# A streaming encoder layer on one NeuronCore: where the conv rows of odd tiles are put in the opening stage, and how x transposed is stored

## What is computed

```
h = rmsnorm(x);  z = h @ w_in            # q, k, v, forget logits, GLU input, memory queries, 3 gates
A = forgetting attention (8 heads x 64)  @ w_fox_o
B = swish(layernorm(causal depthwise conv, width 31, of the GLU)) @ w_conv_o
C = cross attention into 256 memory tokens (4 heads x 128) @ w_mem_o
merged = gate0 * A + gate1 * B + gate2 * C     # gates = sigmoid(h @ w_in[:, C_G:]), 3 x 1024 columns
x = x + merged @ w_out
x = x + PEER(rmsnorm(x))    # 8 heads, top 16 of 128 x 128 experts; rows u[idx], v[idx] of 1024 floats
```

## Time and profile before

| | us |
|---|---|
| device time, median of 3 runs | 4222.19 (4215.44 to 4236.77) |
| device time of the profiled execution | 4211.38 |
| its span, first to last instruction | 4209.6 |
| TensorE busy | 3368.6 (80%) |
| VectorE busy | 2713.5 (64%) |
| GpSimd busy | 2386.7 (57%) |
| ScalarE busy | 1073.8 (26%) |
| data moved | 1321 MB, 314 GB/s on average |

### The profile page before, as it was taken

One profiled execution on the slowest core, in us unless ns is written; L12 is line 12 of the kernel. 1 busy time (PEld: TensorE's weight loads), 2 busy tenths in 40 slices (PEclk: granted clock), 3 DMA queues, 4 the chain that ended last, 5 costly groups with the idle time before them and its releaser, 6 DMA issues.

```text
span 4209.6 us, 34861 instructions
## 1 busy us (share of the span) xinstructions
PE 3368.6 (80%) x9706; PEld 1700.1 (40%) x9706; DVE 2713.5 (64%) x6240; ACT 1073.8 (26%) x2515; POOL 2386.7 (57%) x2341
## 2 busy tenths in 40 slices
PE   8898799897898687777768777776877777687787
PEld 7786454543443343333323333333333333233332
DVE  4599561676776566666666666666666666666674
ACT  5222672223421122112121222212222221222221
POOL 5230340354554366666666666666666666667665
PEclk9999899998999798988989899998988999998998
DMA  6334636798899699999999999999999999999998
GB/s 214 84 90 116 181 109 217 271 315 289 285 343 316 242 363 367 372 360 359 372 362 367 369 367 370 363 372 373 364 368 369 369 366 373 363 378 362 367 362 308
DMA packets 462958, 1321.27 MB, mean 314 GB/s; under 512 B 67802, under 2 KB 134518, under 8 KB 462767
## 3 DMA queue, kind: packets, MB, share of 16 engines
q0 software_dynamic: 313344, 1140.99, 72.1%
q1 hardware_dynamic: 148058, 173.45, 13.1%
q10 hardware_dynamic: 1365, 4.60, 0.3%
HBM read 1275.31 MB, written 43.55 MB: 313 GB/s over the span
## 4 chain that ended last, share of the span: by engine, by line
POOL 22%; PE 13%; issue 12%; DMA 8%; another core or an unknown queue 7%; DVE 5%; ACT 1%; DVEq 0%; POOLq 0%; ACTq 0%
POOL late_u_rows L2129 11%; POOL late_v_rows L2137 11%; PE late_sums_ps L2250 10%; DMA late_u_rows<-in_peer_u,late_expert_idx 4%; DMA late_v_rows<-in_peer_v,late_expert_idx 3%; DVE late_u_rows L2483 2%; PE late_q_ps L2172 1%; PE late_h_T_ps L2154 1%; ACT late_diag L2298 0%; ACT L2287 0%; PE late_h_T_ps L2161 0%; PE late_scores_ps L2188 0%; DVE late_one_hot L2416 0%; DVE late_x L2492 0%
## 5 line engine op out<-in xcount | busy, mean ns | idle before, releaser
L2250 PE MATMUL late_sums_ps<-late_v_rows,late_diag 128*128 128x512 f32 (+1 forms) x3392 | 1742.2, 652 | 487.2 <-DMA late_v_rows<-in_peer_v,late_expert_idx 264.2
L2483 DVE CUSTOM_DVE_ANT_0 late_u_rows<-late_u_rows,late_rows_ps 128x1024 f32<-128x1024 f32 x960 | 1167.3, 1216 | 701.5 <-DMA late_u_rows<-in_peer_u,late_expert_idx 595.9
L2250 PEld LDWEIGHTS late_sums_ps<-late_v_rows,late_diag 128*128 128x128 f32 (+1 forms) x3392 | 655.5, 204 | 1450.8 <-issue 1366.4
L2137 POOL DMA_INDIRECT late_v_rows<-in_peer_v,late_expert_idx x896 | 863.3, 963 | 570.3 <-issue 254.3
L2129 POOL DMA_INDIRECT late_u_rows<-in_peer_u,late_expert_idx x896 | 882.0, 984 | 320.4 <-issue 258.2
L2298 ACT ACTIVATE late_diag<-identity,late_weights 128x128 f32<-128x128 f32 x784 | 271.0, 390 | 798.3 <-DMA open_gain<-in_norm_w 373.5
L1593 POOL DMA_INDIRECT open_u_rows<-in_peer_u,late_expert_idx x128 | 158.4, 1237 | 349.7 <-DVE late_dots L1954 229.2
L2304 ACT ACTIVATE late_gelu<-late_dots 128x4 f32<-128x4 f32 x240 | 48.9, 204 | 971.1 <-issue 577.7
L1968 DVE SCALAR_TENSOR_TENSOR late_x<-open_v_rows,late_weights,late_x 128x1024 f32<-128x1024 f32 x128 | 164.4, 1284 | 115.8 <-issue 94.7
L1128 POOL TENSOR_SCALAR attn_probs<-attn_probs,attn_row_scale 128x256 f32<-128x256 f32 (+2 forms) x68 | 93.2, 1377 | 197.5 <-DVE attn_row_scale L1239 197.4
L481 POOL TENSOR_TENSOR front_w_lower<-front_w_raw,front_w_upper 128x512 fp32r<-128x512 f32 x62 | 95.1, 1553 | 193.2 <-ACT front_w_upper L685 192.0
(11 more groups left out here) (376 smaller groups left out, 4380.3 us busy)
## 6 DMA issues: line engine op xcount, KB each, us to landing
open_weight_columns<-in_w_in SPq DMA_DIRECT2D x96, 256.0 KB
late_u_rows<-in_peer_u,late_expert_idx POOLq DMA_INDIRECT x896
late_v_rows<-in_peer_v,late_expert_idx POOLq DMA_INDIRECT x896
front_w_raw<-in_w_in SPq DMA_DIRECT2D x48, 256.0 KB, 5.6
scr_m<-open_gated SPq DMA_DIRECT2D x42, 256.0 KB
open_weight_columns<-in_peer_w_q SPq DMA_DIRECT2D x32, 256.0 KB
w_mem_o<-scr_m SPq DMA_DIRECT2D x14, 512.0 KB
late_h<-scr_xT SPq DMA_DIRECT2D x12, 512.0 KB
```

Source lines behind the costliest of these rows:

```text
L2137: pool.indirect_dma_start(v[m % V_RING][:], None, io["peer_v"][0], bass.IndirectOffsetOnAxis(ap=rows_of(m), axis=0)).then_inc(s_v[m % V_RI ...
L2250: ins = pe.matmul(acc[0:rows, h, :], diag[k % DIAGS][:, 0:rows], v[n % V_RING][:, h * BANK:(h + 1) * BANK], start=(at == 0), stop=(n == ti ...
L2483: dve.tensor_tensor_reduce(u[n % U_RING][:], u[n % U_RING][:], h2_rows, 1.0, 0.0, ALU.mult, ALU.add, dots[:, n % COLS:n % COLS + 1]).then_ ...
```

## The change

Three edits. The DRAM scratch of x transposed gets a leading tile axis, `(NT + 1, P, KC, P)`, so that a tile of 128 tokens is one run of 1024 floats (4096 bytes) per partition, in the stores of the front and in the loads of the opening (25 loads; for the sample tile, of 64 rows, runs stay 64 floats). The conv rows of odd units go to tile 0's columns of `foxT`. And `load_conv(9)` is issued in SyncE's turn u = 2, after a wait for the routing of head 2, instead of in turn u = 7; the loads of units 10 to 15 stay where they were.

```diff
 def store_whole(xi):
-    sp.dma_start(scr["xT"][:, :, xi * P:xi * P + n], whole[xi % X_RING][:, :, 0:n])
+    sp.dma_start(scr["xT"][xi, :, :, 0:n], whole[xi % X_RING][:, :, 0:n])
...
-conv_rows = [L.memT[:, :, 0:P], w_mem[:, 2, 0:BANK].rearrange("p (j t) -> p j t", j=CT)]
+conv_rows = [L.memT[:, :, 0:P], L.foxT[:, :, 0:P]]
...
 def load_xT(u):
-    sp.dma_start(x_T[u % 2][:, :, 0:rows], scr["xT"][:, :, t * P:t * P + rows])
+    sp.dma_start(x_T[u % 2][:, :, 0:rows], scr["xT"][t, :, :, 0:rows])
...
-sp.dma_start(O.mT[:], scr["xT"][:, :, 0:P])
+sp.dma_start(O.mT[:], scr["xT"][0])
...
 for u in range(UNITS_OPEN):
+    if u == 2:
+        sp.wait_ge(s_done, S0 + 3)
+        load_conv(NT + 1)
     for h in range(2):
         sp.wait_ge(s_ulog, S0 + 2 * u + h + 1)
...
-    if NT <= u + 1 < 2 * NT - 1:
+    if NT <= u < 2 * NT - 2:
         sp.wait_ge(s_uprod, S0 + 2 * u + 2)
         load_conv(u + 2)
...
-("xT", (P, KC, SEQ + SAM))
+("xT", (NT + 1, P, KC, P))
```

More of the change, by code:

```diff
@@ L399, in store_whole @@
                     sp.wait_ge(s_whole, S0 + xi + 1)
-                    sp.dma_start(scr["xT"][:, :, xi * P:xi * P + n], whole[xi % X_RING][:, :, 0:n]).then_inc(s_wout[xi % X_RING], 16)
+                    sp.dma_start(scr["xT"][xi, :, :, 0:n], whole[xi % X_RING][:, :, 0:n]).then_inc(s_wout[xi % X_RING], 16)
                 def load_first():
@@ L1503, in load_xT @@
                     t, rows = unit(u)[1:]
-                    sp.dma_start(x_T[u % 2][:, :, 0:rows], scr["xT"][:, :, t * P:t * P + rows]).then_inc(s_xT[u % 2], 16)
+                    sp.dma_start(x_T[u % 2][:, :, 0:rows], scr["xT"][t, :, :, 0:rows]).then_inc(s_xT[u % 2], 16)
                 def load_conv(u):
@@ L1519, in load_before @@
                     sp.dma_start(merged_before[u % 2][0:rows, :], scr["m"][t - 1, 0:rows, :]).then_inc(s_mold[u % 2], 16)
-                sp.dma_start(O.mT[:], scr["xT"][:, :, 0:P]).then_inc(s_xT0, 16)
+                sp.dma_start(O.mT[:], scr["xT"][0]).then_inc(s_xT0, 16)
                 load_chunk(0)
@@ L1541, in _ @@
                 for u in range(UNITS_OPEN):
-                    p_, t, rows = u // NT, unit(u)[1], unit(u)[2]
+                    t, rows = unit(u)[1:]
+                    if u == 2:
+                        sp.wait_ge(s_done, S0 + 3)
+                        load_conv(NT + 1)
                     for h in range(2):
@@ L2560, in build @@
         ("qT", (HF, 2 * DF + DECAY_ROWS, TOK)), ("kT", (HF, 2 * DF + DECAY_ROWS, PAST + TOK)),
-        ("mqT", (HM, DM, TOK)), ("mkT", (2, HM, DM, NMEM)), ("xT", (P, KC, SEQ + SAM)),
+        ("mqT", (HM, DM, TOK)), ("mkT", (2, HM, DM, NMEM)), ("xT", (NT + 1, P, KC, P)),
         ("y", (CT, P, CONV_OUT)), ("m", (NT + 1, P, D)))}
```

## The result

The changed kernel takes 4213.01 us (median of 20 runs) against 4224.83 us for the kernel before (20 runs): 11.8 us less, ratio 0.9974 with a 95% interval of 0.9965 to 0.9984. One of the 20 runs of the changed kernel was a slow one (4330.74 us at a mean granted clock of 0.846) and is not in the ratio; without it the median is 4212.61 us. The time lies inside the stated range (4186 to 4217), but above the 4211 that the forecast's own ends reach. The gain is 57% of the forecast 20.6 us, and less than the 0.5% that I called measurable from a few runs.

A forecast was written before the change was run, and what follows sets the result against it. In the opening TensorE waits for late conv rows, nothing being at its limit. 17.6 (wait) + 2 (layout) + 1 (start) - 1 (clock) + 1 (end) = 20.6 us, from 4222.2 to 4202 us; range 4186 to 4217.

The forecast's parts named there:

- the forecast's own ends: Whole kernel: main terms taken at their low and high ends, stated as 4193 to 4211 us.
- What bounds: Opening, 970 to 1006 us: nothing at its limit; TensorE waits 19.48 us for unit 9's late conv rows.
- the wait removed: Before `turn_conv(9)`: early load removes 19.48 us idle; with faster matmuls and transposes, 22.4 us by TensorE alone.
- the front: Stores in the front get cheaper, but the weight split behind them was released by ScalarE: 0 us.
- The slower case: Opening: long packets of x hold row gathers longer, costing VectorE 3.0 us per load; 41 us slower, 4263; chance 0.04.
- VectorE late next: Unit 9's norm: VectorE becomes late, so `turn_normed(9)` starts 17.6 us earlier, not 22.4; ends 15.2 and 22.4.
- 2 us from the layout: Whole-tile x loads before unit 9's norm: longer packets save 0.65 us each; VectorE gains 0 to 5.9, taken 2.
- 1 us of the start: Loads ahead of the last query chunk: cheaper tiles give TensorE 0 to 3 us, helping only in part; taken 1.
- an end that brings 1 more: End of the opening: VectorE's last `v` row is late by a DMA; cheaper loads bring 0 to 3 us, taken 1.
- The clock: TensorE idle up to 4.8 us before `turn_normed(9)` slows matmuls behind it: subtract 1 us, ends 0 and 2.5.
- rival two: Late opening: gathers lose their catch-up time; VectorE gains 8 us less than TensorE, which waits; 4210 us; chance 0.17.
- the main case: Whole kernel: the forecast's own case, 20.6 us gained, 4202 us, later conv and fox units keeping their pitch; chance 0.54.

The follow-up runs named there:

- first set: Changed kernel, only the conv rows, only the layout, and changed without conv gate chunks, timed beside the kernel before: 9.4, 11.0, -0.3 and 13.2 us less than its 4209.7.
- second set: Changed kernel with v rows sooner, idle time filled, silu first, or silu first plus sooner v rows: 29.4, 17.8, 31.0, 51.8 us less than the kernel before (3964.1).
- third set: Sooner v rows on the kernel before, on the changed kernel and on conv rows only; changed kernel again: 4.5, 26.6, 17.5, 11.3 us less than before (3961.6).

## Why the prediction was right or wrong

**What bounds, and the wait removed: right.** `turn_conv(9)` lost its 19.48 us, the added load took 0.43 us of SyncE in turn 2, the stretch of low DMA share is full, the front gave nothing (the attention starts at 430.3 us in both kernels). The slower case did not come, nor did a new long wait for a DMA at unit 8; the longest there is 0.85 us.

**VectorE late next: right in kind and nearly in size.** Forecast for unit 9's normed rows: 17.6 us sooner, and with 2 for the loads and 1 for the start 20.6. Measured, counted from the opening's start: 16.0 us (342.0 instead of 358.0), 19.1 and 14.6 in the other two executions, mean 16.6. The kernel before has one profile only, so each of these carries its scatter.

**The step that failed: VectorE was given slack that it doesn't have.** Three terms stood on it: 2 us from the layout, 1 us of the start, and an end that brings 1 more while the rest keeps its pitch. Of the 8.6 us that are missing in the profile (20.6 less 12.0), 4.6 are missing at unit 9 (these two terms, 3, and 1.6 of the 17.6), 3.7 behind unit 15, and 0.3 lies between.

*The layout and the start.* TensorE did reach the first unit 3.5, 4.0 and 2.4 us sooner. All of it was gone at unit 8, where it waited 4.61, 1.95 and 3.50 us for VectorE instead of 0.79. VectorE's step in the memory units took 3.89, 3.82 and 3.86 us against 3.85 before. I had left open whether it is bound by DMA time or by the latency of its ring, and taken a value between. The sooner `v` rows showed that it is mostly the latency, and with it in place the layout's value can't be told from 0 (9.4 us less than before with it, 11.0 without).

**The clock: mis-sized.** I counted one group behind one idle time, 1 us, and 2.5 us given back by the group behind the long wait. There were three idle times and three slow groups in units 8 and 9 (1.70, 1.45 and 1.70 us over 7.03) besides the slow pair behind the wait for gate columns. Over the whole opening the slow groups of sixteen are 7.9 us over 7.03 in the kernel before and 8.4, 8.8 and 9.1 in the three profiles of the changed one: what the clock gave back at one place it took at others. Filling the gaps of five later units gave some 6 us.

**The end: wrong sign.** From unit 15's normed rows (498.1 instead of 512.8, 14.7 us sooner) to the experts the gain fell to 12.0. TensorE lost 1.7 us before its last product, in the second changeover, where it waited 2.2 us in three pieces for gate columns (before: 0.9), and the tail another 1.0 (22.3 us from the last product to the experts, before 21.3). It had been forecast to bring 1. Before:

```profile
1370.14 1.94 PE L2147 MATMUL late_h_T_ps<-identity,late_h 128*128 128x128 f32 x8 [21.34 <-PEq L102]
```

And after:

```profile
1354.78 1.29 DVE L1971 SCALAR_TENSOR_TENSOR late_x<-open_v_rows,late_weights,late_x 128x1024 f32<-128x1024 f32 x1 [2.41 <-DMA open_v_rows<-in_peer_v,late_expert_idx]
...
1363.02 1.94 PE L2150 MATMUL late_h_T_ps<-identity,late_h 128*128 128x128 f32 x8 [22.24 <-PEq L102]
```

The last `v` row is again late by a DMA (2.41 us). This is rival two, the rows that take the gain back, to which I gave 0.17: in the main case I let the rest keep its pitch. In two other executions VectorE's products held TensorE for 1.75 and 4.6 us late in the fox units, where I had read 1.0 us of room. Over the three executions the gain falls from 15.4 us at unit 15's normed rows to 10.6 at the experts. With sooner `v` rows in both kernels nothing of it is lost (19.2 and 19.7), which points at the pace of VectorE's ring here too; why a single execution has more or less of it wasn't tried.

So, in the first profile: 16.0 at unit 9, 1.3 lost by the end of the conv units, 1.7 from there to the last product, 1.0 in the tail, 12.0 left.

**The range: met by its margin.** The low end of the forecast's own case is 15.2 - 2.5 = 12.7 us, which gives 4209.5 and not the 4211 that I wrote; the high end, all terms at their best, gives 4188 and not 4193. The measured gain of 11.8 us lies below that low end of 12.7, and its time is inside 4186 to 4217 only because of what was added for the scatter of the runs and for the rivals.

**The Trainium skill's rule** ("DMA: Bandwidth & Descriptors", Specifications: full line rate from 512 B) made the sum 2 us less, and for the changed kernel that was the better number, but not for the rule's reason: the layout shows no gain there while latency paces VectorE. Where that pace is lifted, longer packets bring 9.1 us by the medians and 4.7 by the profiles, and the rule alone would have said 0.

## What to carry to other kernels

When a long wait goes, ask of every other engine whether it was kept waiting by it too, and whether its own pace (a ring's latency per step, not its busy time) can follow; what it can't follow comes back as short waits on it. Two engines that run side by side at nearly equal pace with hardly a wait between them may both be near the bound, and an edit worth 15 us on one of them can hide behind the other: here sooner gathers were worth 4.5 us alone, the change 12, and both together 27 to 29. Idle time "released by issue" in front of a gather's consumer, summed over a stage, is a line to look at early: here it was the gather. And ask of an edit that wins where else it acts: some 6 us of the sooner gathers came from the last rows of the stage.

## What was not expected of the hardware

Extra matmuls in a 3.6 us gap shortened the groups behind it, which take 8.0 to 9.6 us without them in most cases, to 7.03, and the program by some 6 us.

The same kernel before took 4209.7 us in the first set and 3961.6 in the third, both on the chip numbered 13 (the second set, 3964.1, on number 9), so it is not shown that a different chip is the reason. The mean granted clock differs too (0.915 to 0.925 in the profiles of the first set and of the result, 0.955 to 0.959 in the others), but the profiles place the difference in the experts stage: 2829.6 to 2845.1 us against 2584.1 to 2586.4, while the openings of the changed kernel take 708.4, 709.9 and 715.6. From 1424 to 3900 us the DMA engines moved 366 to 369 GB/s in the three earlier profiles of the kernel before and the changed one, and 406 in the third set's profile of the changed one; TensorE was granted 0.90 to 0.91 and 0.96 there. What limited the rate stays open. Times of different sets can't be compared.

And 4.2 MB fewer bytes on full DMA engines moved VectorE's step only from 4.66 to 4.52 us.
